# Loading the next phase's x tiles and weights during the other-token projection of a hybrid encoder layer

## The reference

```python
h = _rmsnorm(x, rms_gain)                      # over 2048 channels, fp32
proj = jnp.einsum('bsd,de->bse', h, w_in)      # 2048 x 6144
q, k, v, g_a, u_f, g_f = jnp.split(proj, ...)  # six groups of 1024 columns
q = _partial_rope(_rmsnorm(q, q_norm_gain)); k = _partial_rope(_rmsnorm(k, k_norm_gain))
attn = _dilated_attention(q, k, v) * silu(g_a)
four = _fourier_mix(u_f, w_fourier) * silu(g_f)
y = x + jnp.einsum('bse,ed->bsd', concat([attn, four]), w_out)
```

## Time and profile before

| | us |
|---|---|
| median of 2 runs | 2025.2 |
| runs | 2022.4, 2028.0 |
| profiled execution, device time | 2018.7 |
| its span on the slowest core (core 4) | 2017.2 |
| spans of all cores | 1995.2 to 2017.2 |

### The profile page before, as it was taken

One profiled execution on the slowest core, in us unless ns is written; L12 is line 12 of the kernel. 1 busy time (PEld: TensorE's weight loads), 2 busy tenths in 40 slices (PEclk: granted clock), 3 DMA queues, 4 the chain that ended last, 5 costly groups with the idle time before them and its releaser, 6 DMA issues.

```text
span 2017.2 us, 33225 instructions; the slowest of 8 cores (1995.2 to 2017.2 us)
## 1 busy us (share of the span) xinstructions
PE 1752.5 (87%) x12472; PEld 1136.3 (56%) x12472; DVE 567.1 (28%) x768; ACT 589.6 (29%) x998; POOL 324.4 (16%) x233
## 2 busy tenths in 40 slices
PE   1479999359999999999999787887856999999999
PEld 1444588244444444448864376676745888864444
DVE  2753000363333300003410055665531121211221
ACT  3754122464444411110011266666621000000000
POOL 0027000005666600000000122222210000000000
PEclk9579999559999999999999899999878999999999
DMA  6788921766424343456641412122259382249544
GB/s 180 262 175 143 175 49 43 220 193 96 76 56 76 69 82 73 80 102 123 143 98 40 147 48 95 64 82 77 64 91 203 98 195 78 64 82 208 168 149 146
DMA packets 262141, 232.81 MB, mean 115 GB/s; under 512 B 42208, under 2 KB 235872, under 8 KB 254432
## 3 DMA queue, kind: packets, MB, share of 16 engines
q1 hardware_dynamic: 170128, 184.03, 30.0%
q0 software_dynamic: 91856, 46.66, 18.7%
HBM read 218.60 MB, written 58.72 MB: 137 GB/s over the span
## 4 chain that ended last, share of the span: by engine, by line
PE 75%; DMA 9%; ACT 5%; DVE 4%; issue 4%; SPq 3%; POOL 0%; DVEq 0%; ACTq 0%; POOLq 0%
PE ps_pacc L212 44%; PE ps_px L212 10%; PE ps_py L212 8%; PE ps_psc L212 5%; DMA sb_xt<-x_ext 3%; SPq L132 3%; PE ps_pden L212 2%; DMA sb_xr<-x_own 2%; PE ps_pnum L212 2%; DMA sb_xt<-x_own 2%; ACT sb_Vd L236 2%; DVE sb_xn L231 2%; ACT sb_junk L225 1%; PE ps_pvt L215 1%; DMA sb_TB<-dft 1%
## 5 line engine op out<-in xcount | busy, mean ns | idle before, releaser
L212 PE MATMUL ps_pacc<-sb_hT,sb_wbf 128*128 128x512 bf16 x3072 | 680.8, 381 | 1.9 <-DVE sb_hT L237 1.9
L212 PEld LDWEIGHTS ps_pacc<-sb_hT,sb_wbf 128*128 128x128 bf16 x3072 | 301.3, 98 | 367.0 <-issue 7.6
L212 PE MATMUL ps_px<-sb_TB,sb_sdb 128*128 128x256 bf16 x2048 | 233.0, 277 | 35.1 <-DMA sb_sdb<-SDS 29.4
L212 PEld LDWEIGHTS ps_px<-sb_TB,sb_sdb 128*128 128x128 bf16 x2048 | 203.3, 99 | 63.2 <-issue 36.2
L212 PE MATMUL ps_pacc<-sb_wbf,sb_hT 128*128 128x256 bf16 x2048 | 223.9, 273 | 0.0
L212 PE MATMUL ps_py<-sb_wo,sb_mixT 128*128 128x512 bf16 x1024 | 221.5, 379 | 2.3 <-DVE sb_yo L228 1.6
L212 PEld LDWEIGHTS ps_pacc<-sb_wbf,sb_hT 128*128 128x128 bf16 x2048 | 200.4, 98 | 23.6
L215 PE MATMUL ps_ptb<-sb_ident,sb_xn 128*128 128x128 bf16 x640 | 74.3, 308 | 135.0 <-DVE sb_xn L231 61.4
L212 PEld LDWEIGHTS ps_py<-sb_wo,sb_mixT 128*128 128x128 bf16 x1024 | 100.0, 98 | 123.6 <-issue 3.5
L225 ACT ACTIVATE sb_PT<-ps_psc 128x384 bf16<-128x384 f32 (+2 forms) x280 | 127.1, 464 | 86.4 <-PE ps_pden L212 40.6
L132 POOL DMA_DIRECT2D sb_wbf<-w_in x36 | 42.1, 1172 | 671.4 <-PE ps_pacc L212 352.6
(11 more groups left out here) (51 smaller groups left out, 1524.8 us busy)
## 6 DMA issues: line engine op xcount, KB each, us to landing
sb_wbf<-w_in POOLq DMA_DIRECT2D x36, 1024.0 KB, 13.0
sb_xt<-x_ext SPq DMA_DIRECT2D x24, 1024.0 KB, 6.1
sb_xt<-x_own SPq DMA_DIRECT2D x16, 1024.0 KB, 7.0
sb_TB<-dft SPq DMA_DIRECT2D x16, 1024.0 KB, 9.9
sb_xr<-x_own SPq DMA_DIRECT2D x64, 256.0 KB, 3.4
y<-sb_yo SPq DMA_DIRECT2D x64, 256.0 KB, 2.3
KS<-sb_ot SPq DMA_DIRECT2D x64, 128.0 KB, 2.9
VS<-sb_ot SPq DMA_DIRECT2D x64, 128.0 KB, 3.9
```

The lines of the kernel that those rows point to most:

```text
L212: return fw.op(pe, lambda h: h.matmul(out, lhsT=lhsT, rhs=rhs, start=start, stop=stop), R, W, inc)
```

## The change

Four edits. (1) The three `xt` buffers of the own norm are allocated outside (`xtO`), ahead of the other tokens' projection, and their loads of tiles 0 to 2 are issued by a hook at the first block of unit 10 (the third u unit) of that projection; `phase_norm` then skips these three loads. (2) The load of the first own weight unit is issued at the end of that projection's program, ahead of its barrier. (3) To make room, the projection of the other tokens allocates one `ub` and no `uo2`. (4) `gb` is loaded as before, at the start of the norm.

```diff
-        def phase_norm(x_src, hT, ntiles):
+        def phase_norm(x_src, hT, ntiles, xt=None, r_xt=None, preloaded=0):
...
-                xt = [SB(s2, "xt%d" % i, [128, DM], F32) for i in range(NXT)]
-                r_xt = [fw.res() for _ in range(NXT)]
+                if xt is None:
+                    xt = [SB(s2, "xt%d" % i, [128, DM], F32) for i in range(NXT)]
+                    r_xt = [fw.res() for _ in range(NXT)]
...
-                        ld(xt[sl][:], x_src[128 * t:128 * t + 128, :], [r_xt[sl]], key="xt%d" % sl)
+                        if t >= preloaded:
+                            ld(xt[sl][:], x_src[128 * t:128 * t + 128, :], [r_xt[sl]], key="xt%d" % sl)
...
-        def phase_proj(hT, units, rope_d, own, wbf, r_wbf):
+        def phase_proj(hT, units, rope_d, own, wbf, r_wbf, pre_barrier=None, hook=None):
...
-                ub = [SB(s2, "ub%d" % i, [128, 16, 256], BF16) for i in range(2)]
-                r_ub = [[fw.res() for _ in range(2)] for _ in range(2)]
-                uo2 = [SB(s2, "uo%d" % i, [128, 16, 256], BF16) for i in range(2)]
+                nub = 2 if own else 1
+                ub = [SB(s2, "ub%d" % i, [128, 16, 256], BF16) for i in range(nub)]
+                r_ub = [[fw.res() for _ in range(2)] for _ in range(nub)]
+                uo2 = [SB(s2, "uo%d" % i, [128, 16, 256], BF16) for i in range(2)] if own else None
...
                                 if fb:
+                                    if hook is not None and hook[0] == i:
+                                        hook[1]()
                                     if i + NW - 1 < len(units):
                                         load_unit(i + NW - 1)
...
                 run_pipeline(items, [0, 0, 1, 1, 2, 2])
+                if pre_barrier is not None:
+                    pre_barrier()
                 fw.barrier()
...
-            phase_proj(hT, units_o, rope_oth, False, wbfA, r_wbfA)
...
-            prefetch_units(units_w, wbfA, r_wbfA)
-            phase_norm(x_own, hT, 16)
+            with ExitStack() as sXT:
+                xtO = [SB(sXT, "xtO%d" % i, [128, DM], F32) for i in range(3)]
+                r_xtO = [fw.res() for _ in range(3)]
+
+                def pre_x():
+                    for t in range(3):
+                        ld(xtO[t][:], x_own[128 * t:128 * t + 128, :], [r_xtO[t]], key="xt%d" % t)
+
+                def pre_own():
+                    prefetch_units(units_w, wbfA, r_wbfA)
+
+                phase_proj(hT, units_o, rope_oth, False, wbfA, r_wbfA, pre_barrier=pre_own, hook=(10, pre_x))
+                phase_norm(x_own, hT, 16, xt=xtO, r_xt=r_xtO, preloaded=3)
             phase_proj(hT, units_w, rope_own, True, wbfA, r_wbfA)
```

More of the change, by code:

```diff
@@ L407, in s1 @@
                             def s1(t=t, a=a, cs=cs, idx=idx):
-                                uo, r_uo = uo2[idx % 2], r_uo2[idx % 2]
+                                uo, r_uo = (uo2[idx % 2], r_uo2[idx % 2]) if own else (None, None)
                                 if own:
```

## The result

| | before | changed |
|---|---|---|
| undisturbed executions, median | 2024.2 us | 2009.8 us |
| their range | 2021.9 to 2028.7 | 2008.7 to 2010.1 |
| profiled execution, span on the slowest core | 2017.2 (core 4) | 2008.4 (core 6) |

The ratio is **0.9927**, 95% interval 0.9915 to 0.9939, which on 2024.2 us is 14.8 us faster (12.3 to 17.2); by the 2% bound it counts as the same.

What follows compares the result with a forecast made beforehand. TensorE's projection matmuls carry 44% of the span, but the own-token norm waits on DMA loads. Gains of 8.3 us at its start and 4.1 us in its first cycle, 12.4 us, took 2025.2 to 2012.8 us; range 2000 to 2022.

Steps and rivals of the forecast that it cites:

- x tiles and fewer buffers at nothing: Other-token projection: three early x loads hide behind TensorE's work, in by 333.6, and dropping unused buffers costs nothing.
- The signs of being wrong: TensorE stalls in units 10 and 11, barrier later than 363, `gb` after 370, or first cycle well over 11.2 us.
- Weight unit at nothing before the barrier: Other-token projection: the load goes out near 275 and lands by 308, hidden; it gains only by removing norm traffic.
- rival 3: Weight load issued only when the last unit ends, barrier waits: 3.0 us faster to 16.5 us slower; chance 0.03.
- Start of the norm, 8.3 us, set by `gb`: Own norm: tile 0's `sb_xn` starts when `gb` lands, at 368.9 instead of 377.24, gaining 8.3 us.
- First cycle, 4.1 us: Own norm, tile 0 to tile 3: without weight traffic 11.2 us instead of 15.33, gaining 4.1 us.
- the bound of 6.0 us: Most the first cycle could gain, if it fell to 9.4 us, three tiles at 3.12 us each on VectorE.
- Other four cycles unchanged: Own norm, tile 3 to tile 15: stays at 44.8 us; bounds were 7.2 us or 1.5 us of further gain.
- The two terms as independent: Own norm: gains at its start, 8.3 us, and in its first reload cycle, 4.1 us, were added to 12.4 us.
- The rule weighed: Own norm: if POOL's weight load merely starves for descriptors, removing it frees nothing for x tiles; gain 8.3 us, 2016.9.
- Rival 1: Own norm becomes bound by VectorE as loads fall to 4.82 us; gain 19.6 us, 23.2 at the floor; chance 0.13.
- Rivals 2 and 4: 2: only part of the gain, 3 to 9 us, chance 0.18; 4: gain in trace but not time, chance 0.05.

Runs made afterwards that it cites:

- late-load kernel: The changed kernel, but the early weight load waits for the other-token projection's last matmul; 0.9987 (0.9962 to 1.0011), 2.6 us faster than before.

## Why the prediction was right

- **Where the time could move.** Only in the own norm. The stage is 14.1 us shorter in the median over the cores and the time 14.8 (12.3 to 17.2). Forecast 12.4; on core 4, from whose rows it was worked out, the stage went from 83.96 to 71.65 us, 12.3, with 8.3 at the start and 4.2 in the first cycle. That fit to a tenth is partly luck, since the other cores gained 12.0 to 16.8 us.
- **x tiles and fewer buffers at nothing.** Right: TensorE 15.00 of 15 us beside the tiles, and the whole other-token projection 232.8 us before and 232.7 after. The tiles were in by 320.95 on core 6 (forecast by 333.6).
- **The signs of being wrong.** Two of them, read as absolute times, did appear: the barrier opened later than 363 on core 6 (first Square at 363.75), and `gb` landed at 370.16 on core 4. But the own projection's first matmul and everything ahead of the change shift from one execution to the next (first matmul of the other tokens at 124.3 us before and 126.0 after, in the medians). Counted from the end of the phase, the Square came 10.3 us sooner.
- **Weight unit at nothing before the barrier.** Right: it went out at 276.51 on core 6 (forecast near 275) and landed after 14.2 us, not 32.7. The late-load kernel shows what the cover was worth, 7.4 us, and prices rival 3. With 13.2 us of landing the prediction put the net at 3.0 us faster than before. The time, 2.6 us faster, can't confirm it, as its interval includes no gain at all; by the stage the net is 6.7 us, since the first Square came 8.8 us later where 9.4 was taken, and the change itself gains more than the 12.4 that 3.0 was counted from.
- **Start of the norm, 8.3 us, set by `gb`.** Right in mechanism (1.86 us of idle VectorE ended by `gb`, gone when `gb` is early). In size 9.0 us in the median (17.8 to 8.8): `gb` landed in 4.5 to 6.5 us over the cores, median 5.2, where 6.2 was taken (4.5 to 7.2 before, median 6.0). Nothing stood beside it any more, but on core 4 it still took 6.5 us, so what spreads it is open.
- **First cycle, 4.1 us.** Right in mechanism, and under-sized: 5.8 us in the median (16.4 to 10.6). Core 4 had the second-shortest first cycle of the eight (15.33; the others 15.1 to 17.6), so one core's rows understated it. Seen core by core the bound of 6.0 us didn't hold (17.60 to 10.11 on core 3), but the floor under it, 9.4 us for a cycle, did: the shortest is 10.05. With a fourth buffer even the floor fell, to 8.2 us, so 3.12 us isn't VectorE's closest spacing: tiles 0 to 2 of the changed kernel above follow at 2.53 us, before any copy to `hT` comes between.
- **Other four cycles unchanged.** Right: 44.7 and 44.8.
- **The two terms as independent.** This was only partly so. The sum came out, because each was worked out with the other edit in place; taken singly the edits are worth 10.9 and 6.2, not 8.3 and 4.1.
- **The rule weighed.** Without the weight unit the first cycle fell from 16.4 to 10.5 us, and two units slowed two cycles. So the weight load costs the x tiles something, and isn't just late itself. The prediction took "the engines were busy" as proof; the high share alone isn't one, as the queues above show, and the experiments are. The Trainium skill, SBUF — State Buffer, section "SBUF: two separate sides", says that a load issued from POOL can wait for its descriptors while VectorE holds a shared port, with the DMA engines idle. By that rule alone the x tiles would have lost nothing, and these runs disagree.
- **Rival 1** (bound by VectorE) didn't come by fewer transfers; it took a fourth buffer. That kernel gained 22.2 us of stage, within the rival's 19.6 to 23.2, but partly by chance: 8.2 us of it are in the first cycle (5.2 to 5.9 in the rival), because tile 3 no longer waits for tile 0.
- **Rivals 2 and 4** didn't come either: no core's first cycle stayed above 11.6 us, and the gain in the time (14.8) is that of the trace (14.1).

## What to carry to other kernels

Before a barrier that waits for it, a prefetch is free only if it has landed by then: the same load cost nothing when issued some 85 us ahead and 7.4 us when issued at the end. When a buffered loop's time per cycle is load latency plus a chain of engine work, and no engine in it is busy throughout, another buffer pays on top of an earlier start: here 8.1 us for 16 tiles and about 14 for 24, where VectorE had been busy 14.6 to 17.1 of 20 us. And terms should be taken from all cores: the one whose row you read may be at the edge of the spread.

## What was not expected of the hardware

- A weight unit on POOL's queue landed in 10.5 to 15.2 us outside the norm (over the cores of the late-load kernel and the changed one), and needed 32.7 us beside x tiles on core 4. The three reloads of the first cycle took 8.5 to 12.3 us to land beside it (all cores, median 11.0) and 4.8 to 8.1 without it (median 6.7).
- With four buffers, x tiles moved at 334 GB/s at a DMA share of 0.98 on core 0. With three buffers and no weight load the windows above show 252 to 287. All eight cores ran this stage at about the same time after their own start (it began at 353.7 to 362.1 us); the traces don't show whether the starts coincide.
